# Two projection stretches a slot instead of four, and the probabilities' copies behind the next tile's squares

## What is computed

```
u = rms_norm(h) * (1 + scale(c)) + shift(c)
# layer 0: 8 heads, each with two sub-heads of 64
q, k, v, z = split(u @ a_w_in, 4)
q, k = rms_norm per sub-head of 64
p = softmax(q k^T / 8 - slope * dist), causal, for both sub-heads
o = (p1 - lam * p2) @ v ;  o = rms_norm(o) * (1 - lambda_init) * silu(z)
h = h + gate * (o @ a_w_out)
# shared keys and values, 2 heads of 64
k_s, v_s = split(modulated(h) @ w_kv) ;  k_s = rms_norm(k_s)
# layer 1: 16 query heads in 4 groups ("units"), window of 128, a sink logit per head
q, z = split(modulated(h) @ b_w_in) ;  q = rms_norm(q)
p = exp(s - m) / (sum exp(s - m) + exp(sink - m))
h = h + gate * ((p @ v_s * silu(z)) @ b_w_out)
```

## Time and profile before

| | us |
|---|---|
| median of three runs | 1184.56 (1182.88 to 1186.97) |
| the profiled execution | 1183.36 |
| its span, first to last instruction | 1181.6 |
| TensorE busy with matmuls | 1114.6 (94% of the span) |
| VectorE, ScalarE, GpSimd busy | 760.5, 666.3, 151.3 |

### The profile page before, as it was taken

One profiled execution on the slowest core, in us unless ns is written; L12 is line 12 of the kernel. 1 busy time (PEld: TensorE's weight loads), 2 busy tenths in 40 slices (PEclk: granted clock), 3 DMA queues, 4 the chain that ended last, 5 costly groups with the idle time before them and its releaser, 6 DMA issues.

```text
span 1181.6 us, 19499 instructions
## 1 busy us (share of the span) xinstructions
PE 1114.6 (94%) x6120; PEld 887.1 (75%) x6120; DVE 760.5 (64%) x2483; ACT 666.3 (56%) x2041; POOL 151.3 (13%) x293
## 2 busy tenths in 40 slices
PE   1578999999999999999998999989999999999998
PEld 1466777777777777777777788878878778787887
DVE  6786787878878777877877444665555555556222
ACT  4565565666666566665665544666666666666010
POOL 1110111111111111011110111211111111110211
PEclk9988999999999999999999999999999999999999
DMA  9621222322223232222313634301111111113542
GB/s 360 226 81 50 87 73 87 97 64 81 80 90 95 72 100 66 88 81 88 98 54 95 199 102 131 125 19 35 45 43 41 41 41 41 41 50 112 161 143 89
DMA packets 65606, 108.47 MB, mean 92 GB/s; under 512 B 5600, under 2 KB 34400, under 8 KB 65248
## 3 DMA queue, kind: packets, MB, share of 16 engines
q1 hardware_dynamic: 65504, 107.23, 28.8%
HBM read 90.43 MB, written 16.78 MB: 91 GB/s over the span
## 4 chain that ended last, share of the span: by engine, by line
PE 85%; DVE 6%; ACT 3%; issue 3%; DMA 2%; SPq 1%; POOL 0%; DVEq 0%; ACTq 0%; POOLq 0%
PE ps_p L562 15%; PE ps_p L564 14%; PE ps_p L563 14%; PE ps_s L621 6%; PE ps_o L673 6%; PE ps_p L606 5%; PE ps_p L608 5%; PE ps_p L607 5%; PE ps_o L754 4%; PE ps_t L693 3%; PE ps_o L800 2%; PE ps_t L783 2%; PE ps_s L733 2%; DMA ada_in<-ada_w 1%; PE ps_o L647 1%
## 5 line engine op out<-in xcount | busy, mean ns | idle before, releaser
L562 PE MATMUL ps_p<-w_hi,u_hi 128*128 128x512 f32 x768 | 337.7, 440 | 21.9 <-DVE u_lo L1228 21.9
L564 PE MATMUL ps_p<-w_hi,u_lo 128*128 128x512 f32 x768 | 304.5, 396 | 0.0
L563 PE MATMUL ps_p<-w_lo,u_hi 128*128 128x512 f32 x768 | 303.9, 396 | 0.0
L562 PEld LDWEIGHTS ps_p<-w_hi,u_hi 128*128 128x128 f32 x768 | 146.5, 191 | 66.9 <-issue 23.2
L564 PEld LDWEIGHTS ps_p<-w_hi,u_lo 128*128 128x128 f32 x768 | 146.0, 190 | 32.9
L563 PEld LDWEIGHTS ps_p<-w_lo,u_hi 128*128 128x128 f32 x768 | 147.3, 192 | 17.4
L958 ACT ACTIVATE e<-e,negm 128x256 f32<-128x256 f32 (+7 forms) x128 | 98.4, 769 | 82.8 <-DVE negm L1293 81.6
L1182 DVE TENSOR_TENSOR w_lo<-raw,w_hi 128x512 fp32r<-128x512 f32 x120 | 82.8, 698 | 43.0 <-ACT w_hi L869 43.0
L495 POOL TENSOR_SCALAR gbuf<-gbuf 128x128 f32<-128x128 f32 (+1 forms) x96 | 32.9, 343 | 541.9 <-ACT gbuf L896 541.9
L995 ACT ACTIVATE pT<-ps_t 128x512 f32<-128x512 f32 (+2 forms) x96 | 44.5, 490 | 75.1 <-PE ps_t L693 74.6
L673 PE MATMUL ps_o<-va,pT 128*128 128x128 f32 x576 | 78.4, 281 | 0.0
(11 more groups left out here) (184 smaller groups left out, 2148.9 us busy)
## 6 DMA issues: line engine op xcount, KB each, us to landing
adabuf<-ada_w SPq DMA_DIRECT2D x48, 512.0 KB, 3.9
raw<-w_a SPq DMA_DIRECT2D x76, 256.0 KB, 3.9
raw<-w_b SPq DMA_DIRECT2D x44, 256.0 KB, 3.1
ada_in<-ada_w SPq DMA_DIRECT2D x7, 1024.0 KB, 13.4
x_in<-x SPq DMA_DIRECT2D x8, 512.0 KB, 12.5
oa_scratch<-gbuf SPq DMA_DIRECT2D x64, 64.0 KB, 1.6
late<-oa_scratch SPq DMA_DIRECT2D x8, 512.0 KB, 4.5
stage<-x SPq DMA_DIRECT2D x8, 512.0 KB, 4.9
```

Of the source, the lines that this page charges most:

```text
L562: pe.matmul(o, u_hi[:, c, t], w_hi[par][:, c, :], start=(c == 0), stop=False)
L563: pe.matmul(o, u_hi[:, c, t], w_lo[par][:, c, :], start=False, stop=False)
L564: mm = pe.matmul(o, u_lo[:, c, t], w_hi[par][:, c, :], start=False, stop=(c == KD - 1))
```

## The change

Two things change. On TensorE the projection of a slot comes in two stretches. With `cut = 3` where the tile has a second score piece and 4 where it has none (always 4 in B), chunks 0 to cut-1 stand behind the first score piece, and chunks cut to 7 behind the transposes of q and k; the stretch of chunk 3 between the values' product and these transposes, and the stretch of chunk 7 behind the transposes of the probabilities, are gone, so that the projection of a slot ends before the probabilities are transposed. On ScalarE the copies of the probabilities move from the end of slot s to slot s+1, behind `head_of_tile` and ahead of `rsqrt_seed`. What is computed stays the same.

```diff
@@ TensorE, attention A
+                    cut = 3 if len(score_chunks(i3)) > 1 else 4
+
...
-                    part_of_projection(range(0, 3))
+                    part_of_projection(range(0, cut))
...
-                    part_of_projection(range(3, 4))
                     if live(2) and s > 2:
                         queries_and_keys()
-                    part_of_projection(range(4, 7))
+                    part_of_projection(range(cut, KD))
...
-                    part_of_projection(range(7, KD))
@@ TensorE, attention B
-                    part_of_projection(range(0, 3))
+                    part_of_projection(range(0, 4))
...
-                    part_of_projection(range(3, 4))
...
-                    part_of_projection(range(4, 7))
+                    part_of_projection(range(4, KD))
...
-                    part_of_projection(range(7, KD))
@@ ScalarE, attention A (in B alike)
                     if live(2):
                         head_of_tile(S, P, live, s, i2)
+                    if live(4):
+                        for k, (c0, c1) in enumerate(score_chunks(i4)):
+                            act.wait_ge(S.pt, UNIT_CHUNKS * u4 + SCORE_CHUNKS[i4] + k + 1)
+                            last = act.activation(pT[:, c0:c1], ps_t[:, c0:c1], ACT.Copy)
+                        last.then_inc(S.phi, 1)
                     if not (isinstance(u, int) and u == 0 and i < 2):
                         rsqrt_seed(S, s, 5)
...
                     split_for(S, u, i, par, live, units, U_A)
                     if not live(0) and i == 4:
                         transposed(n0, 1)
-                    if live(3):
-                        for k, (c0, c1) in enumerate(score_chunks(i3)):
-                            act.wait_ge(S.pt, UNIT_CHUNKS * u3 + SCORE_CHUNKS[i3] + k + 1)
-                            last = act.activation(pT[:, c0:c1], ps_t[:, c0:c1], ACT.Copy)
-                        last.then_inc(S.phi, 1)
```

More of the change, by code:

```diff
@@ L964, in slot @@
                     i2, i3, i4 = (i - 2) % 8, (i - 3) % 8, (i - 4) % 8
-                    u3 = u + (i - 3) // 8
+                    u3, u4 = u + (i - 3) // 8, u + (i - 4) // 8
                     if live(2):
                         head_of_tile(S, P, live, s, i2)
+                    if live(4):
[3 more added lines that the diff above has]
+                        last.then_inc(S.phi, 1)
                     if not (isinstance(u, int) and u == 0 and i < 2):
@@ L1062, in slot @@
                     n2, n3, n4 = s - 2, s - 3, s - 4
-                    i2, i3 = (i - 2) % 8, (i - 3) % 8
+                    i2, i3, i4 = (i - 2) % 8, (i - 3) % 8, (i - 4) % 8
                     first = u == 0
@@ L1070, in slot @@
                         head_of_tile(S, 256, live, s, i2)
+                    if live(4):
+                        act.wait_ge(S.pt, n4 + 1)
+                        for g in range(2):
+                            w0 = P if i4 == 0 else 0
+                            o, src = (v[:, g * 512:(g + 1) * 512].rearrange("p (j c) -> p j c", c=256)[:, :, w0:256]
+                                      for v in (pT, ps_t))
+                            last = act.activation(o, src, ACT.Copy)
+                        last.then_inc(S.phi, 1)
+                    if live(2):
                         rsqrt_seed(S, s, 4)
@@ L1103, in slot @@
                         transposed(n0, 1)
[L1104 to L1111, removed]
                 all_units(act, units, 5, slot)
```

## The result

| | before | after |
|---|---|---|
| median, us | 1184.35 (1182.88 to 1186.97, 4 runs) | 1170.25 (1167.90 to 1173.55, 4 runs) |
| ratio, with its 95% interval | | 0.9893 (0.9868 to 0.9918) |
| profiled execution, us | 1183.36 | 1173.55 |
| its span, mean granted clock | 1181.6, 0.991 | 1171.8, 0.991 |

The change makes the kernel 1.1% faster: 12.7 us by the ratio, where 5.2 were forecast and 1173 was the low end of the range. The sign was right, the size was not. Three single executions behind this document took 2212 to 2805 us, at a mean granted clock of 1.000, and are left out of every median and ratio.

A forecast was written before the change was run, and what follows sets the result against it. TensorE, with 85% of the chain that ended last, was taken as the bound. Terms 0 + 2.4 + 2.1 + 0.7 + 0 + 0 = 5.2 us put the median 1184.56 at 1179.4, stated as 1179; range 1173 to 1186.

The forecast's parts named there:

- part 1: TensorE's merged projection stretches: seams to short groups cost nothing; term 0, bounds +-1 us over 94 projecting slots.
- Part 2: Probabilities' transposes one chunk later in A: tiles 6 and 7 stop waiting for combined exponentials; 2.4 us, bounds 0 and 3.
- part 3: ScalarE's squares come earlier: waits at tile 0 of B's units go, tile 1's stay; 2.1 us, bounds 1 and 2.9.
- part 4: First slots of B: an eighth chunk fills 0.69 of the wait for key rows' transposes; 0.7 us, bounds 0 and 0.8.
- part 5: Copies ahead of ScalarE's seed of the roots: delay covered, in B by 1.5 us against 1.08; cost 0.
- part 6: First unit of A: copy leaves the modulation loop, x's rows are transposed one chunk later; term 0, bounds -3 and +3.
- rival B: The seams are real, an apparent 0.09 us each: 17 + 5 us gained, 1163 to 1168 us; chance 0.07.
- rival C: Waits in A's tiles 6 and 7 only move, to the second score piece's maxima: 1182 to 1184 us; chance 0.26.
- Rival E: Longer runs of transposes lower TensorE's clock once a unit, 18 us: 1197 to 1203 us; chance 0.03.

The follow-up runs named there:

- the kernel before again: The kernel before, unchanged, run once more for another profile: 1178.07 us.
- the control: The changed kernel, unchanged, run once more beside three further kernels: 1171.91 us against 1182.69 of the kernel before, ratio 0.9917.
- chunk 3 alone: The kernel before with only chunk 3 (last chunk in A's two-chunk tiles) joined to the stretch before the values' product: 1183.67 us against 1183.62, ratio 0.9991.

## Why the prediction was wrong

The step that failed is part 1's: a seam was put at nothing, +-1 us, and the merged seams gave 2.2. A second step failed beside it: half clock at the end of A stood in no term of the sum and gave 1.5. Part 2 was right in its mechanism and too small.

One pair of traces has first units of nearly one length, the kernel before again (span 1176.3) and the control (1166.4). Its 9.9 us, beside the prediction's parts:

| | forecast | measured | shown by |
|---|---|---|---|
| part 1, seams | 0 | 2.2 | B's 1.2: chunk 3 alone gave 1.1 of it; A's 1.0 only by distances |
| part 2, tiles 6 and 7 of A, six units | 2.4 | 2.9 | gone with the last chunk and the copies |
| part 3, tile 0 of B | 2.1 | 2.4 | gone with the last chunk and the copies, 0.2 of it with chunk 3 |
| part 4, first slot of B | 0.7 | 0.7 | the same |
| part 5, the copies | 0 | 0 | TensorE's order alone is 1.8% slower |
| part 6, first unit | 0 | -0.2 | varies by 5 us in either kernel |
| end of A | none | 1.7 | three traces of each; 1.5 of it half clock |
| slot 94 | none | 0.2 | |

**Part 1 failed.** "A seam to a short group thus costs nothing" rested on one distance for each kind of group, 0.11 a short matmul by division. The step back to the projection costs 0.09 (0.32 for 0.23), as the long L562 had suggested; about half of it is given back where short matmuls follow one another. Of the two seams one is worth 0.053 a slot in B and the other 0.000. So rival B's 0.09 for every seam was wrong as well. The error was in the bound: +-0.01 a slot was narrower than the division allows. A short matmul at 0.11, rounded, leaves 0.005 open, and times sixteen that is 0.08, about as much as the seam itself. A's 1.0 is the rest in tiles 0 to 5: in tile 2, 7.47 became 7.41, in tile 3, 7.95 became 7.91. Tile 4 is the only one that got longer, by 0.03. Chunk 3 alone doesn't bring the 1.0; with the last chunk and the copies moved, chunk 3's move is 0.5 of it (463.41 to 462.90). Where the other half comes from stays open.

**Part 2 was right in kind and undersized.** The stall of tile 7 has a part ahead of its first transpose. TensorE's timeline of the kernel before again, tile 7:
```profile
558.62 0.48 PE L562 MATMUL ps_p<-w_hi,u_hi 128*128 128x512 f32 x1
...
560.84 1.32 PE L693 MATMUL ps_t<-ident,e 128*128 128x128 f32 x8
561.91 0.47 PE L562 MATMUL ps_p<-w_hi,u_hi 128*128 128x512 f32 x1
```
Eight transposes take 1.07, 0.28 over the 0.79 of the earlier trace rows's kind, as forecast. The nine long matmuls ahead take 560.84 - 558.62 = 2.22, where those of tile 6 take 2.13. That 0.09 was missed: I took the distance from the first transpose, which had itself waited. Tile 7 lost 0.38 and gained it all back, tile 6 0.10, not 0.07. In a unit that is 0.48, not 0.35. (The first unit's share stands in the row of part 6.) No wait took its place, so rival C fell; the combination is just in time now (562.17), with nothing to spare.

**Parts 3 and 4 held.** In the earlier trace rows's terms the maxima of tile 0 are no longer late (1.60 behind the first score, 927.73 and 926.13, for 2.75 before, 937.72 and 934.97), tile 1's waits stayed as said (0.8 us, three times), and 0.7 was the first slot's gain to 0.02. In the profiled execution the squares stand 0.77 ahead of the scores (925.36, 926.13) and stood 0.38 behind them (935.35, 934.97): 1.15 earlier, a little more than the 0.9 forecast.

**Part 5's cover held.** In B the seed is ready at 927.45 + 0.21 and Newton starts at 929.13, so 1.5 us of cover were left at tile 0. Slot lengths in A show no loss but tile 4's 0.03. What would have happened without the copies' move wasn't asked in the prediction: 31 us separate that kernel from the changed one (1203.26 to 1171.91, the control), so each half of the change is worth little or less than nothing alone (1178.40, 1203.26).

**Part 6 and the clock.** The first unit's term was right as a mean (84.1 in the three traces of either kernel), but two executions can differ by 5, and its bounds were 3. In the profiled pair it gave 1.2. But the prediction counted half clock only there. A stretch under matmuls at the end of A stood in the trace of before and wasn't priced; in the kernel after it costs nothing any more, and that gave 1.5. No row of before tells where a stretch will fall after a change, so the rows could give a bound for it, not the 1.5.

**Rival E fell.** Half clock stood behind waits of TensorE, not behind transposes; not every wait brought it (617 to 620 in the kernel after: 1.25 busy of 3.00, and 1.00 in the 20 us behind it). The window 780 to 1050 of the kernel after, with the longer run of short matmuls in each slot:
```profile
780.00:1050.00 270.00, 268.81 (x1611) 222.96 (x1610) 143.81 (x575) 170.70 (x575) 33.60 (x58) 1.00 0.14 41
```
TensorE's new order with the copies late has the same transposes and does fall to half clock, behind its longest waits.

The parts and the end of A explain the 9.9 of this pair and the control's ratio (0.9917, 9.8 us). The four runs of the result gave 12.7 with an interval of some 3 to either side; what is over 10 in them is left as the spread of executions, since no trace shows a structural place for it.

## What to carry to other kernels

Where an engine in order copies what another produces late, moving the producer's end and moving the copy are one change: alone the first made this kernel 1.8% slower, the second 0.3% faster, together they made it 0.8 to 1.1% faster. A stall read from a group of matmuls has a second part ahead of the group's first start; compare the distance before it as well. Before saying that a seam costs nothing, carry the rounding of a divided number back through its count, and that through the number of slots: 0.08 a seam and 94 slots were 7.5 us here, not 1. Once there are two kernels, compare the whole repeated slot, which resolves 0.001 us, rather than a pair of neighbours.

## What the runs showed of the hardware

- One kernel's first unit lasts anything from 81.4 to 86.5 us, with stretches at half granted clock in changing places, while the steady slot of B repeats to 0.001 us. One such stretch under dense matmuls costs about 1.5 us (7.30 to 8.74 in slot 94 of the kernel after, 161.0 to 162.5 at the end of A). The Trainium skill (TensorE: Matmul & The Clock Gate, Part 1) calls the number of matmuls at the lower clock at a kernel's start different from run to run; here the same holds for stretches far behind the start, and the first unit alone is a spread of 0.4% for this kernel.
- Two seams of the same kind differ. Sixteen matmuls of 128x64 directly before two transposes save 0.053 us a slot against three long matmuls between them, which then stand at the end of a run of long ones; eight transposes directly before eight score matmuls save 0.000 against the same three.
